# Rotary queries of the second block, made feature-major instead of token-major and transposed

## The reference, cut to what matters

```
u = rms_norm(h, pre_mix_gain)
qa, ka, va, qb, kb, vb, g = split(u @ w_in_2)       # qa, qb: 1024 columns each
qa, ka, qb, kb = rope(each, pos)                    # heads of 64: x1*cos - x2*sin, x2*cos + x1*sin
o_swa  = windowed attention of 16 heads of qa over 4 key heads, 16 meta tokens and a sink
o_diff = 8 heads of (softmax(q1 k1) - lam * softmax(q2 k2)) @ vb, normalised
merged = sigmoid(g_a) * (o_swa @ w_a) + sigmoid(g_b) * (o_diff @ w_b);  h += rms_norm(merged @ w_out)
```

## Time and profile before

| what | value |
|---|---|
| median of 3 runs | 882.3 us (881.87 to 884.05) |
| profiled execution, its own time | 885.11 us |
| its span in the trace | 883.5 us |
| granted TensorE clock | 0.999 |
| busy PE / DVE / ACT / POOL | 99% / 70% / 52% / 5% of the span |
| DMA read from HBM | 151.58 MB |

### The profile page before, as it was taken

How to read it: one execution, slowest core, us unless ns; L and a number is a source line. 1 busy time by engine, 2 the same in 40 slices (tenths; PEclk the granted TensorE clock), 3 DMA queues, 4 the chain that set the end, 5 groups by cost and what they waited for, 6 DMA issues and landing times.

```text
span 883.5 us, 12940 instructions
## 1 busy us (share of the span) xinstructions
PE 872.8 (99%) x4790; PEld 731.8 (83%) x4790; DVE 622.5 (70%) x994; ACT 459.4 (52%) x742; POOL 45.1 (5%) x81
## 2 busy tenths in 40 slices
PE   8999999999999999999999999999999999999997
PEld 5887788888888888889998777777888888888886
DVE  5876677666876666668855788887766876666665
ACT  5636633434644444454556666677643654444443
POOL 0100000000200000002000000123300100000000
PEclk9999999999999999999999999999999999999999
DMA  9956344554565555453673223423365265555531
GB/s 344 361 206 218 99 159 166 185 186 159 183 238 192 190 191 191 142 186 110 199 260 116 96 102 114 168 96 125 114 246 186 99 237 188 187 194 188 187 143 47
DMA packets 24733, 154.64 MB, mean 175 GB/s; under 512 B 2912, under 2 KB 4192, under 8 KB 7280
## 3 DMA queue, kind: packets, MB, share of 16 engines
q1 hardware_dynamic: 22224, 146.61, 46.9%
q10 hardware_dynamic: 2464, 7.42, 2.6%
HBM read 151.58 MB, written 1.05 MB: 173 GB/s over the span
## 4 chain that ended last, share of the span: by engine, by line
PE 95%; DVE 3%; ACT 1%; DMA 1%; issue 0%; DVEq 0%; ACTq 0%
PE ps L477 21%; PE ps L479 20%; PE ps L478 20%; PE ps L598 15%; PE ps L602 8%; PE ps L1514 2%; PE ps L1440 1%; PE ps L1188 1%; PE ps L1464 1%; DMA h<-x_tiles 1%; DVE sc L1824 1%; PE ps L617 1%; PE ps L1459 0%; DVE wlo L1625 0%; ACT sc L963 0%; PE ps L1454 0%
## 5 line engine op out<-in xcount | busy, mean ns | idle before, releaser
L1625 DVE TENSOR_TENSOR wlo<-raw,whi 128x2048 fp32r<-128x2048 f32 x134 | 306.6, 2290 | 148.4 <-ACT whi L704 147.9
L704 ACT ACTIVATE whi<-raw 128x2048 fp32r<-128x2048 f32 x134 | 256.4, 1915 | 182.8 <-PE ps L479 114.4
L477 PE MATMUL ps<-whi,xT 128*128 128x512 f32 (+1 forms) x224 | 88.5, 395 | 0.0
L479 PE MATMUL ps<-whi,xT 128*128 128x512 f32 (+1 forms) x224 | 85.8, 383 | 0.0
L478 PE MATMUL ps<-wlo,xT 128*128 128x512 f32 (+1 forms) x224 | 85.6, 382 | 0.0
L598 PE MATMUL ps<-x_all,whi 128*128 128x512 f32 x336 | 80.0, 390 | 0.0
L598 PEld LDWEIGHTS ps<-x_all,whi 128*128 128x128 f32 x336 | 62.3, 188 | 12.5
L477 PE MATMUL ps<-whi,x_all 128*128 128x512 f32 x160 | 65.8, 411 | 0.4 <-ACT qbT L970 0.2
L479 PE MATMUL ps<-whi,x_all 128*128 128x512 f32 x160 | 62.7, 392 | 0.0
L478 PE MATMUL ps<-wlo,x_all 128*128 128x512 f32 x160 | 62.4, 390 | 0.0
L598 PE MATMUL ps<-xT,whi 128*128 128x512 f32 x256 | 61.6, 391 | 0.0
(11 more groups left out here) (323 smaller groups left out, 1620.2 us busy)
## 6 DMA issues: line engine op xcount, KB each, us to landing
raw<-weights SPq DMA_DIRECT2D x134, 1024.0 KB, 4.8
raw<-weights SPq DMA_DIRECT2D x3, 512.0 KB, 7.6
cst<-consts SPq DMA_DIRECT2D x1, 1499.0 KB, 13.7
kswap<-kraw SPq DMA_DIRECT2D x20, 68.0 KB, 2.0
gate_a<-gain_rows ACTq DMA_DIRECT2D x2, 512.0 KB, 5.4
gate_r<-gain_rows ACTq DMA_DIRECT2D x2, 512.0 KB, 5.6
gate_s<-gain_rows ACTq DMA_DIRECT2D x2, 512.0 KB, 8.1
gate_d<-gain_rows ACTq DMA_DIRECT2D x2, 512.0 KB, 5.2
```

Source lines behind the costliest of these rows:

```text
L477: pe.matmul(o, lh, rh, start=first, stop=False)
L479: return pe.matmul(o, ll, rh, start=False, stop=last)
L704: act.activation(whi[s][:], raw[s][:], ACT.Copy).then_inc(split_hi, 1)
L1625: dve.tensor_tensor(wlo[s][:], raw[s][:], whi[s][:], ALU.subtract).then_inc(split_lo, 1)
```

## The change

Queries get the treatment that keys had. Every blob of 256 query columns is multiplied with its weights held still (`multiply_queries`: for each of two 128-column tiles, 8 products of 512 columns, which take the high and low part of the tokens together, and 8 of 256). ACT copies the low sums out (`queries_low`), DVE adds them to the high sums into `kraw` (`queries_raw`), SP's queue swaps halves of heads, and DVE rotates (`turned_queries`). The blobs at places 6, 7 and 12 to 17 are the query blobs, and each blob of the stage from 1 to 17 uses one pair of banks in turn. The transposes, ACT's copies after them, `rope_whole` for these heads, `tok2` and the tables `h_cos` and `h_sin` go. `turn` gets a place of its own in SBUF.

```diff
-TURNED = (3, 6, 7, 8)
-TURN_AT = {16: ((0, 0), (0, 1)), 28: ((1, 0),), 30: ((1, 1),), 32: ((2, 0),), 34: ((2, 1),), 36: ((3, 0),), 38: ((3, 1),)}
+QUERIES = (6, 7, 12, 13, 14, 15, 16, 17)
+SWAPPED = (0, 1, 2, 3, 4) + QUERIES
+def query_made(U):
+    cc, _ = unit_place(U)
+    return 6 + U // S_UNITS * 4 + cc // 2
...
+        def multiply_queries(pe, slot, bank, j):
+            for k in range(KC):
+                pe.matmul(ps[:, bank + j, :], vh[:, k, j * P:(j + 1) * P], x2[:, :, k, :], start=k == 0, stop=False)
+            for k in range(KC):
+                m = pe.matmul(ps[:, bank + j, 0:TOK], vl[:, k, j * P:(j + 1) * P], x2[:, 0, k, :],
+                              start=False, stop=k == KC - 1)
...
-            def turn_keys(i):
-                sp.wait_ge(taken_a, taken_by(16 + i))
+            def swap_halves(m2):
+                sp.wait_ge(taken_d if m2 in QUERIES else taken_a, taken_by(16 + m2))
...
             for n in range(N1, plain):
                 load(n, w[n], n - 2)
-                if n in (N1 + 4, N1 + 5, N1 + 6, N1 + 7, N1 + 8):
-                    turn_keys(n - N1 - 4)
+                if n - N1 - 4 in SWAPPED:
+                    swap_halves(n - N1 - 4)
...
+            def queries_low(m2):
+                act.wait_ge(blob_used, N1 + m2 + 1)
+                if m2 - 2 in SWAPPED:
+                    act.wait_ge(kt_ok, SWAPPED.index(m2 - 2) + 1)
+                act.activation(kraw[b][:, :, 0:TOK], ps[:, bank:bank + 2, TOK:2 * TOK], ACT.Copy).then_inc(ql_ok, 1)
...
# ACT, body q
                 if q in (2, 4, 6, 8, 10):
                     keys_out(q // 2 - 1)
+                if q % 2 == 0 and m - 1 in QUERIES:
+                    queries_low(m - 1)
...
-                for r, t in TURN_AT.get(q - 1, ()):
-                    act.wait_ge(q_ps, turned(r, t))
-                    act.activation((qsT if r < 2 else qbT)[...], ps[:, turn_bank(r, t), :]..., ACT.Copy).then_inc(q_ok, 1)
...
# PE
-                for r, t in TURN_AT.get(q - 1, ()):
-                    pe.wait_ge(rope_ok, turned(r, t))
-                    for j in range(4):
-                        m = pe.transpose(ps[:, turn_bank(r, t), j * P:(j + 1) * P], tok2[r % 2][...], ident)
-                    pe.wait_ge(q_ok, turned(U // 8, t))
-                    if U == 0:
-                        pe.wait_ge(q_ok, turned(0, 1))
-                        pe.wait_ge(kt_ok, 5)
+                    pe.wait_ge(kt_ok, query_made(U))
+                        if m2 in QUERIES:
+                            multiply_queries(pe, slot_of(n), pair_bank(m2), part)
...
# DVE
+            def queries_raw(m2):
+                dve.wait_ge(ql_ok, QUERIES.index(m2) + 1)
+                dve.tensor_tensor(raw_q, ps[:, bank:bank + 2, 0:TOK], raw_q, ALU.add).then_inc(taken_d, 2)
+
+            def turned_queries(m2):
+                dve.wait_ge(taken_d, taken_by(16 + m2))
+                dve.wait_ge(ks_in[b], 64 * (swaps_before(m2) + 1))
+                dve.tensor_tensor(raw_q, raw_q, cs, ALU.mult)
+                link(dve, "dve", dve.tensor_tensor(swap_q, swap_q, sn, ALU.mult))
+                dve.tensor_tensor(dst, raw_q, swap_q, ALU.add).then_inc(kt_ok, 1)
...
# DVE, body q: ahead of unit_front, and last
+                if q % 2 == 0 and m2 - 1 in QUERIES:
+                    queries_raw(m2 - 1)
...
-                for r, t in TURN_AT.get(q, ()):
-                    rope_whole(tok2[r % 2][:, t, :], ..., rope_ok, scratch2, stat[:, t, 3:4])
+                if q % 2 == 1 and m2 - 1 in QUERIES:
+                    turned_queries(m2 - 1)
```

More of the change, by code:

```diff
@@ L70 @@
                       ("zero_end", N_META), ("pad", 6),
-                      ("h_cos", NT * DH), ("h_sin", NT * DH),
                       ("gt", P), ("diag1", P), ("ret_cos", NT * P), ("ret_sin", NT * P),
@@ L103, in xt_made, with pair_bank, values_blob, swaps_before @@
     return 2 * KC * r + 2 * XT_ORDER[r].index((t, k // 2 * 2)) + k % 2 + 1
-TURNED = (3, 6, 7, 8)
-TURN_AT = {16: ((0, 0), (0, 1)), 28: ((1, 0),), 30: ((1, 1),), 32: ((2, 0),), 34: ((2, 1),), 36: ((3, 0),), 38: ((3, 1),)}
+QUERIES = (6, 7, 12, 13, 14, 15, 16, 17)
+SWAPPED = (0, 1, 2, 3, 4) + QUERIES
 VALUES_AT = {12: 0, 18: 1, 20: 2, 22: 3, 24: 4}
[L113 to L120, removed]
+def pair_bank(m2):
+    return 2 * ((m2 + 1) % 2)
+def values_blob(i):
+    return 7 + i if i else 5
+def swaps_before(m2):
+    return len([m for m in SWAPPED if m < m2 and m % 2 == m2 % 2])
 def unit_place(U):
     return U % S_UNITS // 8 * 4 + U % 4, U % 8 // 4
-def turned(r, t):
-    return 4 + 2 * r + t + 1
+def query_made(U):
+    cc, _ = unit_place(U)
+    return 6 + U // S_UNITS * 4 + cc // 2
 def slot_of(n):
@@ L282, in build @@
         gate_d = at("gate_d", [P, NT, D], F32, region)
-        tok2 = [new("tok2a", [P, NT, 512]), new("tok2b", [P, NT, 512])]
+        top[0] = region + NT * D
         vs = new("vs", [P, NT, S_KV * DH])
@@ L293, in build @@
         sT_h = new("sT_h", [P, KC, TOK], F32R)
-        turn = at("turn", [P, 2, KEYS], F32, top[0])
         sT_l = new("sT_l", [P, KC, TOK], F32R)
@@ L298, in build @@
         pmT = new("pmT", [P, P])
-        scratch2 = new("scratch2", [P, 512])
+        scratch2 = new("scratch2", [P, 2 * DH])
+        turn = new("turn", [P, 2, KEYS])
         o_tok = [at("o_tok0", [P, P], F32, dead + KC * TOK), new("o_tok1", [P, P]), new("o_tok2", [P, P])]
@@ L397, in build @@
         kt_ok = sem("kt_ok")
+        ql_ok = sem("ql_ok")
         ks_in = [sem("ks_in0"), sem("ks_in1")]
@@ L445, in build @@
         TAKERS = "aadd" + "aa" + "dd" + "dddd" + "dd" + "dd" + (
-            "aaaaa" + "a" + "d" + "aaaa" + "d" + "dd" + "dddd" + "dd" + "dd")
+            "aaaaa" + "a" + "dd" + "aaaa" + "dd" + "dddd" + "dddd" + "dd" + "dd")
         def wait_pair_free(pe, group):
@@ L604, in multiply_wide @@
             m.then_inc(blob_used, 1)
+        def multiply_queries(pe, slot, bank, j):
+            vh = whi[slot][:].rearrange("p (k c) -> p k c", k=KC)
+            vl = wlo[slot][:].rearrange("p (k c) -> p k c", k=KC)
+            for k in range(KC):
[3 more added lines that the diff above has]
+                              start=False, stop=k == KC - 1)
+            if j == 1:
+                m.then_inc(blob_used, 1)
         def multiply_by_tile(pe, slot, bank0, x, made, between):
@@ L673, in _ @@
             load(N1 - 1, w[N1 - 1], N1 - 1 - 3)
-            def turn_keys(i):
-                sp.wait_ge(taken_a, taken_by(16 + i))
-                b = i % 2
+            def swap_halves(m2):
+                sp.wait_ge(taken_d if m2 in QUERIES else taken_a, taken_by(16 + m2))
+                b = m2 % 2
                 for g in range(4):
@@ L680, in turn_keys @@
                     sp.dma_start(kswap[b][o:o + 32], kraw[b][s:s + 32]).then_inc(ks_in[b], 16)
-            plain = N1 + 12
+            plain = N1 + 24
             for n in range(N1, plain):
                 load(n, w[n], n - 2)
-                if n in (N1 + 4, N1 + 5, N1 + 6, N1 + 7, N1 + 8):
-                    turn_keys(n - N1 - 4)
+                if n - N1 - 4 in SWAPPED:
+                    swap_halves(n - N1 - 4)
             whole = (NBLOB - plain) // 3 * 3 + plain - N1
@@ L918, in keys_out @@
                                    ACT.Copy).then_inc(taken_a, 1)
-            def values_out(i):
[L923 to L926, removed]
+            def queries_low(m2):
+                b, bank = m2 % 2, pair_bank(m2)
+                act.wait_ge(blob_used, N1 + m2 + 1)
+                if m2 - 2 in SWAPPED:
+                    act.wait_ge(kt_ok, SWAPPED.index(m2 - 2) + 1)
+                act.activation(kraw[b][:, :, 0:TOK], ps[:, bank:bank + 2, TOK:2 * TOK], ACT.Copy).then_inc(ql_ok, 1)
+            def values_out(i):
+                m2 = values_blob(i)
+                b, bank = m2 % 2, pair_bank(m2)
+                act.wait_ge(blob_used, N1 + m2 + 1)
+                if m2 - 2 in SWAPPED:
+                    act.wait_ge(kt_ok, SWAPPED.index(m2 - 2) + 1)
                 act.activation(kraw[b][:], ps[:, bank:bank + 2, 0:KEYS], ACT.Copy).then_inc(v_raw, 1)
@@ L931, in values_in @@
                 act.wait_ge(v_ps, i + 1)
-                pair = ps[:, values_bank(i):values_bank(i) + 2]
+                bank = pair_bank(values_blob(i))
+                pair = ps[:, bank:bank + 2]
                 if i == 0:
@@ L967, in _ @@
                     ins.then_inc(u_exp, 1)
-                for r, t in TURN_AT.get(q - 1, ()):
-                    act.wait_ge(q_ps, turned(r, t))
-                    act.activation((qsT if r < 2 else qbT)[:, 4 * (r % 2):4 * (r % 2) + 4, t * P:(t + 1) * P],
-                                   ps[:, turn_bank(r, t), :].rearrange("p (j q) -> p j q", j=4),
-                                   ACT.Copy).then_inc(q_ok, 1)
                 U = q - U0 - 2
@@ L1015, in _ @@
                     g = (q - 43) // 4
-                    act.wait_ge(taken_d, taken_by(16 + 14 + g))
```

(53 more changed lines are left out.)

## The result

The changed kernel takes 888.0 us in the median (885.96 to 888.63, 6 runs) where the kernel before takes 883.17 in the runs beside it (881.87 to 884.56, 6 runs). The ratio of the two is 1.005, with an interval from 1.0036 to 1.0064: about 4.4 us slower (the medians alone are 4.8 apart), where +4.0 was forecast. The time itself, 888.0, lies above the forecast's own range (885.1 to 887.6) and inside the wider one (881.5 to 888.5); 0.9 us of that distance is the kernel before, which takes 883.17 here and 882.3 in the runs that the forecast started from. PE is busy for 868.5 us instead of 872.8, and yet the kernel takes longer.

The account below looks back on a forecast made before the run. PE and DVE were taken as level in the units' stage, with DVE to become the bound. Early transposes -0.79, early blobs +0.16, to slot 38 +5.1, last transposes -0.44: +4.0 on 882.3, 886.3 us; range 885.1 to 887.6, wider 881.5 to 888.5.

Parts of the forecast that it names:

- DVE's round decides: In the units' stage, DVE's longer round stalls PE; scores of slot 38 start +5.1 us later.
- The size of the round: DVE's round over two slots in the units' stage: 11.51 us against PE's 10.02, bounds 10.55 and 11.73.
- PE's first wait: At the scores of slot 28: due at 500.38, they start at 501.0 because `u_max` comes at 500.94.
- PE's terms: On PE's path: transposes -3.43 us, their waits -0.4, dearer products +0.64; -3.2 if only these count.
- the early transposes less the early products: Before the units' stage: transposes after slot 16 save 0.79 us, products of early blobs 6 and 7 cost 0.16.
- The price of a query blob: Products on PE: 5.55 us in the new form against 5.47, 0.08 more per blob, 0.64 for 8.
- DMAs and SP at nothing: 32 added swap DMAs land 4.4 us after `queries_raw`, wanted 8.9 after it; with SP's waits they cost nothing.
- ACT's copies at nothing: On ACT, eight `queries_low` replace eight copies of the same size (0.57 us each): nothing in busy time.
- the cover named for it: DVE's rotation covers ACT's `queries_low`; without it each would put its 0.5 us ahead of `queries_raw`.
- PE as the bound: Rival: PE stays the bound, only its terms count, -3.2 us to 879.1; chance 0.17.
- The order of ACT: Rival: `hi` ready sooner than F + 5.64, round 10.6 to 11.2, total 881.5 to 884.8 us; chance 0.20.
- The late swap: Rival: swap DMAs land over 6.5 us after the last issue, delaying rotation, 890 us and more; chance 0.03.

Follow-up runs that it names:

- both moves: Changed kernel with the rotation moved to the end of the next even DVE body and `queries_raw` moved between `unit_front` and `unit_back`: 879.06 us, ratio 0.9945.
- its experiment: Changed kernel with ACT's `hi` put ahead of the scaling of probabilities in even bodies of the windowed units: ratio 0.9982 to the kernel before.
- the rotation late: Changed kernel with the rotation moved from the end of its odd DVE body to the end of the next even body: ratio 1.0026 to the kernel before.
- raw in the gap: Changed kernel with `queries_raw` moved from ahead of `unit_front` to between `unit_front` and `unit_back` in even bodies: ratio 1.0000 to the kernel before.

## Why the prediction was right, step by step

*DVE's round decides.* Shown from both sides: less DVE work gives the time back at 1 to 1, more takes it, and moving the same work without changing its amount takes 7.3 us out of block 2 (from +3.55 to -3.79).

*The size of the round.* Forecast 11.51, measured 11.45: `lo` at F + 5.64 exactly, rotation 1.93 (1.94), `queries_raw` 0.60 (0.65 taken between 0.60 and 0.77). PE's first wait was 0.42 us instead of some 0.6, the four after it 1.36 to 1.40 instead of 1.49. The scores of slot 38 come 4.12 us later after block 2's start (554.16 - 396.46 against 552.79 - 399.21), where the forecast's terms give +4.5. Behind them it is -0.57 against -0.44.

*PE's terms.* Up to slot 22 block 2 gained 0.79, where the early transposes less the early products give 0.63. The price of a query blob was sized well. In the changed kernel one reads

```profile
439.59 2.00 PE L616 MATMUL ps<-x_all,whi 128*128 128x512 f32 x8
441.43 1.11 PE L618 MATMUL ps<-x_all,wlo 128*128 128x256 f32 x8
442.38 2.00 PE L616 MATMUL ps<-x_all,whi 128*128 128x512 f32 x8
444.23 1.12 PE L618 MATMUL ps<-x_all,wlo 128*128 128x256 f32 x8
445.18 0.29 PE L482 MATMUL ps<-x_all,whi 128*128 128x272 f32 x1
```

5.59 us (445.18 - 439.59) where 5.55 was taken from the feed-forward. But the price is a difference to the old form, and in the units' stage it shows in PE's undisturbed round: 10.00 (both moves) against 9.94 before, 0.06 a blob where 0.08 was taken. The Trainium skill (TensorE: Matmul & The Clock Gate, "Back-to-back issue gap") gives N / 2.4 + 2.5 ns for one isolated product; an estimate by it puts the 8 wide products at 1.73 us and the 8 narrow ones at 0.87. The rows show about 1.85 and 0.95, so this case decides against that formula for its stream of products.

*DMAs and SP at nothing.* Right in block 2's length, by the experiment without them. *ACT's copies at nothing.* Right in the changed kernel, and the cover named for it was the true one: taken away, 0.76 us a round came out.

*The rivals.* PE as the bound did not come; it is what both moves make. The order of ACT was a true lever (its experiment turns the loss into a gain) but needs a change of the code: `whi` did not come sooner by itself. The late swap did not come either: without the swap nothing changed.

The Trainium skill (VectorE: DVE Perf Modes, "The TRN2 errata") has 691 ns for such an addition. Rows agree as a busy time (0.68 to 0.69) and not as a distance: starts are 0.60 apart, and 0.72 where a link stands between (the second operation waits for a semaphore that the first one raises).

How much of the number is luck? The mechanism and the round came as forecast, but +4.0 lies between two measures that differ: block 2 grew by 3.55 in one pair of executions, the ratio of the runs says 4.4. The errors in block 2 all go one way, PE's first five waits some 0.1 to 0.2 shorter than forecast and the gains on PE some 0.1 to 0.2 larger.

What stays open: why the runs differ by about 0.9 us more than block 2 does, why the version with both moves is 0.6 us (by the ratio 1.7) better than PE's terms, and why the stretch from the merged gates to the end is 0.12 to 0.25 us shorter than before in all nine kernels, without any change in it.

## What to carry to other kernels

An engine's mean busy share does not say whether it has room. Write its round in the stage in question as a chain with all its waits, and compare that with the bounding engine's round. Before you move work in an engine's fixed order, ask which waits it covers where it stands and where it will stand: here the same two pieces, moved into the engine's own waits, turned +0.5% into -0.55%. When profiled spans disagree with medians, compare from a mark behind the unchanged part.

## What the hardware showed that I had not expected

The start of the kernel varies by more than most edits bring. The six times of the kernel before beside the result lie in two groups (881.87 to 882.3 and 884.05 to 884.56), but the 22 and 29 runs beside the experiments fill the space between and reach 886.39, so the groups are no rule. The profiled executions of the ten kernels, whose first block is the same code, reach block 2 between 396.46 and 399.21 us. Nearly all of that arises ahead of PE's first true product: from it to block 2 take 387.9 to 388.5 us in all ten. In the profile before, PE's first transposes wait for the tokens to 7.22, and its first true product, with weights, starts at 10.74:

```profile
7.22 1.09 PE L1188 MATMUL ps<-cst,h 128*128 128x128 f32 x4 [2.43 <-DMA h<-x_tiles]
...
10.74 0.92 PE L477 MATMUL ps<-whi,xT 128*128 128x512 f32 x1
```

In the changed kernel they start at 5.18 and 8.53:

```profile
5.18 0.63 PE L1211 MATMUL ps<-cst,h 128*128 128x128 f32 x4 [0.44 <-DMA h<-x_tiles]
...
8.53 0.47 PE L482 MATMUL ps<-whi,xT 128*128 128x512 f32 x1 [1.01 <-DVE xT L1662]
```

The landing of the first tokens differs by 2 us, and in the former the same four transposes take 1.09 us instead of 0.63 and the first product 0.92 instead of 0.47. Both count: with the rotation late the tokens land later than with raw in the gap (transposes at 6.85 against 6.60), but its transposes take 0.63 instead of 1.09, and its first product starts sooner (9.11 against 9.87). The granted clock reads 1.00 over the first 12 us in all ten traces, so it does not tell the two kinds of start apart. What makes a start the one or the other was not tested.
